# The mLSTM input projection of an encoder layer moved ahead of the attention and computed from the split x

## The reference, cut to what matters

```python
z = x @ w_in + b_in
(a_x, a_g, sb_q, sb_k, sb_v, ml_q, ml_k, ml_v, ml_o, ml_i, ml_f, mg) = jnp.split(z, offs, axis=-1)
# branch A: conv -> RG-LRU(a_x) * gelu(a_g)        branch B: stick-breaking attention(sb_q, sb_k, sb_v)
# branch C: mLSTM(ml_q, ml_k, ml_v, ml_i, ml_f) -> headwise LayerNorm * ml_norm_g * sigmoid(ml_o)
mixed = g[:, :, 0] * (ya @ w_pa) + g[:, :, 1] * (yb @ w_pb) + g[:, :, 2] * (yc @ w_pc)   # g = sigmoid(mg)
x = _layer_norm(DN_ALPHA * x + mixed @ w_out, ln1_g, ln1_b)
```

## Time and profile before

| what | value |
|---|---|
| median of 3 runs | 2867.72 us (2865.27 to 2868.11) |
| the profiled execution's own time | 2888.07 us |
| its span | 2886.3 us |
| TensorE (PE) busy | 2605.4 us, 90% of the span |
| VectorE (DVE) / ScalarE (ACT) / GpSimd (POOL) busy | 1564.3 / 1324.7 / 624.7 us |
| mean granted TensorE clock | 0.952 of full speed |
| data moved | 442.00 MB, 153 GB/s |

### The profile page before, as it was taken

The page is one execution under the profiler, slowest core; times in us unless marked ns, Lnnn a source line. Parts: engine busy times, 40 slices in busy tenths (PEclk is TensorE's granted clock), DMA queues, the critical chain, the costliest instruction groups (busy, mean ns, idle before and its releaser), DMA issues. The chain is left out here.

```text
span 2886.3 us, 40166 instructions
## 1 busy us (share of the span) xinstructions
PE 2605.4 (90%) x14952; PEld 2256.1 (78%) x14952; DVE 1564.3 (54%) x2508; ACT 1324.7 (46%) x2057; POOL 624.7 (22%) x494
## 2 busy tenths in 40 slices
PE   6997898889999699999989886599999999999991
PEld 5996687654447599999987565499999999899990
DVE  3655215653105644544534364477777777777774
ACT  3665214432013333434332222267677776777762
POOL 1000003301102001011113222133433334343333
PEclk9998899999999799999999888799999999999995
DMA  4110313192001455555534311588888888888864
GB/s 127 53 55 19 122 48 117 56 361 70 0 29 16 88 127 138 143 135 136 139 105 153 116 44 48 180 249 255 276 244 276 257 265 274 247 274 249 276 199 157
DMA packets 372397, 442.00 MB, mean 153 GB/s; under 512 B 20509, under 2 KB 299925, under 8 KB 372282
## 3 DMA queue, kind: packets, MB, share of 16 engines
q1 hardware_dynamic: 352264, 379.29, 42.3%
q0 software_dynamic: 15680, 50.90, 7.4%
q10 hardware_dynamic: 4338, 10.23, 0.9%
HBM read 389.36 MB, written 51.01 MB: 153 GB/s over the span
## 5 line engine op out<-in xcount | busy, mean ns | idle before, releaser
L2979 PE MATMUL banks<-slot_rowsT,expert_w_high 128*128 128x384 f32 x2048 | 603.2, 363 | 0.4 <-DVE slot_rowsT L3080 0.4
L2981 PE MATMUL banks<-slot_rowsT,expert_w_low 128*128 128x192 f32 x2048 | 515.0, 251 | 0.0
L2981 PEld LDWEIGHTS banks<-slot_rowsT,expert_w_low 128*128 128x128 f32 x2048 | 392.3, 192 | 1.3
L2979 PEld LDWEIGHTS banks<-slot_rowsT,expert_w_high 128*128 128x128 f32 x2048 | 385.5, 188 | 2.0 <-issue 0.6
L3015 ACT CAST expert_w_high<-expert_w 128x2048 fp32r<-128x2048 f32 x128 | 238.0, 1908 | 21.2 <-DMA expert_w<-in_exp_w 21.2
L3074 DVE TENSOR_TENSOR expert_w_low<-expert_w,expert_w_high 128x2048 fp32r<-128x2048 f32 x96 | 216.9, 2285 | 22.0 <-ACT expert_w_high L3015 22.0
L2884 POOL TENSOR_TENSOR expert_w_low<-expert_w,expert_w_high 128x2048 fp32r<-128x2048 f32 x32 | 147.6, 4613 | 264.1 <-ACT expert_w_high L3015 264.1
L1926 PE MATMUL banks<-xT_chunk_high,w_gates_high 128*128 128x384 f32 x576 | 193.5, 336 | 11.0 <-DVE xT_chunk_low L1992 11.0
L1927 PE MATMUL banks<-xT_chunk_low,w_gates_high 128*128 128x384 f32 x576 | 193.3, 336 | 0.0
L1928 PE MATMUL banks<-xT_chunk_high,w_gates_low 128*128 128x384 f32 x576 | 193.3, 336 | 0.0
L3140 DVE TENSOR_TENSOR expert_w_low<-expert_w,expert_w_high 128x1024 fp32r<-128x1024 f32 x128 | 157.0, 1227 | 54.4 <-ACT expert_w_high L3044 53.5
(11 more groups left out here) (482 smaller groups left out, 6043.7 us busy)
## 6 DMA issues: line engine op xcount, KB each, us to landing
expert_w<-in_exp_w SPq DMA_DIRECT2D x128, 1024.0 KB
expert_w<-in_exp_w SPq DMA_DIRECT2D x32, 2048.0 KB, 10.8
w_gates<-in_w_in SPq DMA_DIRECT2D x72, 512.0 KB, 4.5
cached_k<-in_cache_sb_k SPq DMA_DIRECT2D x16, 1024.0 KB, 9.0
cached_v<-in_cache_sb_v SPq DMA_DIRECT2D x16, 1024.0 KB, 10.9
w_proj<-in_w_pa SPq DMA_DIRECT2D x24, 512.0 KB, 5.2
w_ax_ag<-in_w_in SPq DMA_DIRECT2D x16, 512.0 KB, 4.7
w_sb_piece<-in_w_in SPq DMA_DIRECT2D x24, 256.0 KB, 3.7
```

The source lines that it names most:

```text
L2979: nc.tensor.matmul(out[:, 0:2 * SLOTS], hi, xgT[:, par, k].rearrange("p a s -> p (a s)"), start=(k == 0), stop=(k == DT - 1), skip_group_c ...
L2981: last = nc.tensor.matmul(out[:, 0:SLOTS], lo, xgT[:, par, k, 0, :], start=False, stop=(k == DT - 1), skip_group_check=True)
```

## The change

The mLSTM projection is moved to directly behind `stage_lru`, where `x_hi` and `x_lo` are still in SBUF, and works in three-term products. Its outputs go to DRAM scratch (q and k^T by feature, k, v and o by token) and `stage_mlstm` loads them back in four groups of tiles. The second load and turn of x are gone. For the merge gates GpSimd adds `x_hi` and `x_lo` during `stage_lru` and stores the sum to DRAM (`xT_d`), and `stage_mix` loads it by chunks into one buffer `xa` that later in the chunk holds `ya`. The blank halves of `qz` and the ones of `v_aug` are written by VectorE at the start of `stage_mlstm`.

```diff
 def stage_lru(nc, g, x_hi, x_lo, xT):
...
+            for k in range(DT):
+                if k >= H:
+                    pool.wait_ge(x_out[k % H], 16)
+                pool.tensor_tensor(xT[:, k % H, :], x_hi[:, k, :].bitcast(F32), x_lo[:, k, :].bitcast(F32), ALU.add
+                                   ).then_inc(x_joined, 1)
+                pool.wait_ge(x_joined, k + 1)
+                pool.dma_start(g.xT_d[k], xT[:, k % H, :]).then_inc(x_out[k % H], 16)
...
+def stage_ml_project(nc, g, x_hi, x_lo, turn, m):
+    pieces = [(s, k) for s in range(3) for k in range(DT)]
+    offs = (O_MO, O_MQ, O_MV)
+    RAW, WR, NBK, R = 4, 12, 6, 3
+    QK = [(c, tile) for c in range(len(CHUNKS3)) for tile in (2, 3, 0, 1)]
...
+        GATE_PARTS = (((0, 384), (384, 768)), ((768, 960), (960, T)))
...
+            for n in range(DT, WR + RAW):
+                load(n)
+            for i in range(NT - 1):
+                store_o(i)
+            sp.wait_ge(m_ready, 1)
...
+            for n in range(WR + RAW, 2 * DT + RAW):
+                load(n)
+            store_o(NT - 1)
+            for c in range(2):
+                store_features(c)
+            for n in range(2 * DT + RAW, 3 * DT):
+                load(n)
+            store_features(2)
...
+            for i in range(NT):
+                sp.wait_ge(tok_moved, NT + i + 1)
+                sp.dma_start(g.mv_d[i], tok[:, (NT + i) % R, :]).then_inc(tok_out[(NT + i) % R], 16)
...
+            for i in range(NT):
+                token_rows(0, i, i)
+                if 1 <= i <= 2:
+                    gates(i - 1)
+            for u, (c, tile) in enumerate(QK):
...
+                if u == 2:
+                    turn_gates()
+                if u % 4 == 3:
...
+                    for i in range(3 * c, 3 * c + 3):
+                        turn_k(i)
+            for i in range(NT):
+                token_rows(2, NT + NQK + i, i)
...
+        @block.vector
...
+            for t in range(NT - 1):
+                move(t)
+                if t == 2:
+                    running_rows()
+                if t == 4:
+                    exponents()
+            for n in range(WR, 2 * DT + 4):
+                weight_low(n)
...
+        @block.scalar
...
+            for i in range(2, 5):
+                sigmoid(i)
+            act.wait_ge(rows_ready, 1)
...
+            for i in range(5, NT - 1):
+                sigmoid(i)
+            for n in range(WR, 2 * DT + 4):
+                weight_high(n)
...
-class XRows:
-def stage_turn_rows(nc, g, rows, rows_in, xT):
-def stage_ml_project(nc, g, xT, m):
...
 def stage_mlstm(nc, g, m, ycT):
+        GROUPS = ((0, 1), (1, 3), (3, 6), (6, NT))
...
+            for n, (first, end) in enumerate(GROUPS):
+                cols = slice(first * P, end * P)
+                for half in range(2):
+                    r = slice(64 * half, 64 * half + 64)
+                    sp.dma_start(m.qz[r, half::2, cols], g.mq_d.rearrange("a p t -> p a t")[r, :, cols]
+                                 ).then_inc(tiles_in[n], 16)
+                sp.dma_start(m.kT[:, :, cols], g.mkT_d.rearrange("a p t -> p a t")[:, :, cols]
+                             ).then_inc(tiles_in[n], 16)
+                sp.dma_start(m.k_tok[:, first:end, :], g.mk_d.rearrange("i p d -> p i d")[:, first:end, :]
+                             ).then_inc(tiles_in[n], 16)
+                for i in range(first, end):
+                    last = sp.dma_start(m.v_aug[:, i, :, 0:HD], g.mv_d[i].rearrange("p (h e) -> p h e", h=H))
+                    last.then_inc(tiles_in[n], 16)
...
+                tiles_loaded(pe, i)
+                if i < 2:
+                    pe.wait_ge(blank, 2 + 2 * i)
...
 def stage_mix(nc, g, mixT, yb, yc):
                 sp.dma_start(wg[:, n % 2], w_in_t[:, :, O_MG + r * D + m * P:O_MG + r * D + (m + 1) * P]
                              ).then_inc(wg_in[n % 2], 16)
+                if n == 0:
+                    load_x(0)
...
+                if n % U == 2 * DT + 2 and c + 1 < C:
+                    sp.wait_ge(y_split, 4 * H * (c + 1))
+                    load_x(c + 1)
                 if n % U == 3:
-                    if c:
-                        sp.wait_ge(y_split, 4 * H * c)
-                    sp.dma_start(ya[:], g.yaT_d.rearrange("k p t -> p k t")[:, :, c * CHUNK3:(c + 1) * CHUNK3]
+                    sp.wait_ge(x_split, DT * (c + 1))
+                    sp.dma_start(xa[:], g.yaT_d.rearrange("k p t -> p k t")[:, :, c * CHUNK3:(c + 1) * CHUNK3]
                                 ).then_inc(ya_in, 16)
```

More of the change, by code:

```diff
@@ L308, in stage_lru @@
         states_out = sem("a_states_out")
+        x_joined = sem("a_x_joined")
+        x_out = [sem(f"a_x_out{i}") for i in range(H)]
         block = ctx.enter_context(nc.Block())
@@ L1588, in stage_mlstm @@
         seg = sb("request_mask", [P, NB])
+        GROUPS = ((0, 1), (1, 3), (3, 6), (6, NT))
+        group_of = [n for n, (lo, hi) in enumerate(GROUPS) for i in range(lo, hi)]
+        tiles_in = [sem(f"r_tiles_in{n}") for n in range(len(GROUPS))]
+        o_in = sem("r_o_in")
+        blank = sem("r_blank")
+        ones_ready = sem("r_ones_ready")
         c_in = sem("r_c_in")
@@ L1794, in new_state @@
                 last.then_inc(c_ready, 1)
+            for cols in (slice(0, P), slice(P, T)):
+                for half in range(2):
+                    nc.vector.memset(m.qz[64 - 64 * half:128 - 64 * half, half::2, cols], 0.0).then_inc(blank, 1)
+            nc.vector.memset(m.v_aug[:, :, :, HD:HD + 1], 1.0).then_inc(ones_ready, 1)
             for i in range(NT):
@@ L1896, in _, with load_x @@
             w_in_t = g.w_in[0].rearrange("(k p) n -> p k n", p=P)
+            def load_x(c):
+                for half in range(2):
+                    k = slice(4 * half, 4 * half + 4)
+                    sp.dma_start(xa[:, k, :], g.xT_d.rearrange("k p t -> p k t")[:, k, c * CHUNK3:(c + 1) * CHUNK3]
+                                 ).then_inc(x_in[half], 16)
             for n, (c, r, m) in enumerate(units):
@@ L2025, in _ @@
                 first = n % U < DT
-                if first:
-                    dve.wait_ge(x_split, DT * (c + 1))
                 out = mixT[:, m, c * CHUNK3:(c + 1) * CHUNK3] if first else sig[:, n % RING, :]
@@ L3310, in build_program @@
                     prompt.close()
[L3311 to L3315 removed]
+                    stage_sb_sample(nc, g, qT, k_new, v_new, cache)
                 cache.close()
```

629 lines of the change are left out of this document (354 added, 275 removed).

## The result

The kernel after takes 2830.82 us (median of 4 runs, 2828.16 to 2833.89), the kernel before in the same batch 2867.91 us (4 runs). The ratio is 0.9874, 95% interval 0.9861 to 0.9886: faster by 37.1 us. The forecast was 2830.0 us, range 2816 to 2851. The profiled execution took 2832.34 us, with a span of 2830.6.

The account below looks back on a forecast made before the run. TensorE, busy 90% of the span, bounds dense stretches; stage edges count elsewhere. -231.0 + 183.8 + 1.5 + 4 + 4 = -37.7 us; against the median of 2867.72 that gives 2830 us, range 2816 to 2851.

Parts of the forecast that it names:

- Removed and added: Second turn of x and float32 projection go, -231.0 us; the new projection stage before the attention costs 183.8 us.
- The late gate chain: New projection stage: ScalarE's casts come in time by 1 to 2 us; rival: late, +8 us, 2838, chance 0.12.
- GpSimd in the LRU stage: LRU stage: eight GpSimd additions slow two or three VectorE operations by 0.5 us each, +1.5 us.
- the lock rival: LRU stage: GpSimd's additions lock VectorE out, at most five on the path, +13.5 us for 1.5, 2842; chance 0.08.
- Start of the mLSTM stage: mLSTM stage: first reload group takes 5 to 7.5 us before score matmuls, +4 us, ends 0 and 10.
- Start of the mix: Mix: 1.5 MB of x stand ahead of the first projection weights, +4 us, between +2 and +8.
- Slow reloads: Rival, mLSTM stage: q, k, v reloads crawl at 50 GB/s, 61 us for 4, 2887; chance 0.10.

Follow-up runs that it names:

- second profiles: Kernel before and kernel after each run once more unchanged, for a second profile: 2868.37 us and 2831.95 us.
- experiment 7: Kernel after with additions spread over the LRU stage, mix's first projection weights ahead of x, and four casts ahead of the gates' exponentials: 2823.13 us.
- experiment 4: Kernel after with a GpSimd memset of 2.68 us in place of each addition, storing only the high part of x: 2830.12 us in one run.
- experiment 2: Kernel after with each GpSimd addition held back until an LRU output tile is done, spreading them over the stage: 2825.40 us, ratio to before 0.9851.
- experiment 3: Kernel after without GpSimd's additions, storing only the high part of x: 2826.09 us, ratio 0.9861.
- experiment 6: Kernel after with the mix's first projection weights issued ahead of the first chunk of x: 2829.82 us, ratio 0.9867.
- experiment 1: Kernel before plus only GpSimd's eight additions and their stores in the LRU stage, result unread: 2875.32 us against 2868.52, ratio 1.0024.

## Why the prediction was right

The sum was -37.7 us and the runs gave -37.1, but it is a hit in which some of the terms missed and made up for each other. The terms against both pairs of profiles, in us (the mix is taken up to the next stage's first issue; the 22.75 us of the late weights are taken off the first pair's later stages):

| | forecast | first profiles | second profiles |
|---|---|---|---|
| LRU stage | +1.5 | +9.4 | +8.8 |
| new projection | +183.8 | +184.9 | +184.9 |
| attention | 0 | +1.6 | +0.5 |
| second turn and float32 projection | -231.0 | -231.0 | -233.0 |
| mLSTM stage | +4 | +1.4 | -1.6 |
| mix | +4 | +3.8 | +4.3 |
| later stages | 0 | -3.1 | -0.3 |
| sum | -37.7 | -33.0 | -36.4 |

Term by term, against the first profiles where nothing else is said:

- **Removed and added: right.** -231.0 stands. The new stage was put at 183.8 us and takes 184.9. Its parts: start 4.2 us for 4.4; first nine tiles and gates 66.2 for 66.6; features with the turns and waits 60.9 for 59.3; last nine tiles 49.6 for 48.6; end 4.1 for 4.4. The rows of the attention's own projection are good prices for the new one.
- **The late gate chain: nearly free.** I gave a margin of 1 to 2 us and no cost. The group row of the new stage shows a wait of 1.4 us at the first feature unit:

```profile
L796 PE MATMUL banks<-xT_high,w_ml_high 128*128 128x384 f32 x96 | 33.6, 350 | 1.4 <-DVE w_ml_low L826 1.4
```

  ScalarE reached the casts 66.6 us after the first matmul, where I had 66; TensorE's fifth piece would have been wanted at 68.3 instead of 69.4 and came 0.5 us late, the sixth 0.9. (The forecast's own numbers, 66.6 and twelve matmuls of 175 ns, give 68.7 and not 69.4.) With four casts ahead of the exponentials (experiment 7) the wait is gone. The loss of 8 us was never near.
- **GpSimd in the LRU stage: the step that failed.** "Two or three VectorE operations on that path at 0.5 us each give +1.5 us" should have read: each is shut out until GpSimd's whole instruction ends, up to 2.7 us, and TensorE, idle for 6.8 us, comes back at half clock. The stage grew by 9.4 us for 1.5; by the experiments 5 to 7 us of that reach the time. VectorE operations of over 2.5 us early in this stage were named beforehand as the sign of a wrong step, and they are there. The mechanism is that of the lock rival, which had a chance of 0.08; its price of 13.5 us was too high, as the rows shut out on the convolution's path add up to 6 us, with 2.8 us of half clock behind them. I called the row beside it, 0.5 us longer at the median, milder than the rule of the Trainium skill's page (experiment 4), and I took from that rule only the operations with two SBUF inputs, while two of the three stretched rows have a single tensor as input. The row is not milder. The operations beside that row in the trace of before show why:

```profile
1105.43 1.02 POOL L2039 TENSOR_TENSOR xT<-xT,gate_sigmoid 128x384 f32<-128x384 f32 x1 [7.04 <-DVE gate_sigmoid L2030]
...
1105.81 1.72 DVE L2008 TENSOR_TENSOR w_gates_low<-w_gates,w_gates_high 128x1024 fp32r<-128x1024 f32 x1 [0.46 <-ACT w_gates_high L1962]
```

  GpSimd's addition there is of 384 columns and 1.02 us long, and 0.64 us of it were left when the split began. The split lost 0.5 us because little more was left to wait for; beside an addition of 2.7 us the same wait is up to 2.7 us. The units of the mix without an addition have splits of 1.22 us. A loss per operation can't be carried over to another stage without the length of what stood beside it.
- **Start of the mLSTM stage: the loads cost little.** I took +4 us for 4.48 to 8.5 us up to the first score matmul. They began 5.95 us in, 7.04 in the second profile, against 4.48 and 5.66 in the two of before. In its first 5 us TensorE has sixteen small matmuls that need no load, in either kernel, and only what comes after them waits for one. That wait is none in the first profile of after, 1.17 us in the second, 0.2 to 1.1 in experiments 2, 3 and 6:

```profile
848.53 2.08 PE L1787 MATMUL banks<-ycT,ml_kT 128*128 128x128 f32 x8 [1.17 <-DMA ml_v<-ml_v_scratch]
```

  So of the 1.4 us between the second profiles 1.2 are this wait. Of the 1.5 us between the first profiles it is nothing: there the small matmuls take 5.8 us at half clock and took 4.4 us in the kernel before, where they began at full clock. The stage takes 109.5 and 110.0 us after, 108.05 and 111.56 before: the change costs between -2.1 and +1.9 us, by which pair one takes.
- **Start of the mix: right.** +4 forecast, +4.1 measured, from 7.97 to 12.09 (+3.4 in the second profiles, from 7.96 to 11.40), by the very order of the list. The x chunk and the weights behind it arrive by 962.4.
- **Slow reloads: wrong rival.** 268 GB/s.

The two pairs differ by 3.4 us in the sum, and the two profiles of before reach the mix 5.9 us apart. That is more than the 0.6 us by which the forecast missed the runs, so such a hit is partly luck: 7 to 8 us of the LRU stage were missed, and 3 to 6 us that the mLSTM stage did not cost, with what the other stages differ by between executions, made up for them. What was shown is the new stage's price, the loss in the LRU stage, and the mix's start.

## What to carry to other kernels

Price a new stage by the twin that already stands in the trace, down to start and end; that held within 1.1 us of 184. When work is moved to GpSimd because it is idle, look at what VectorE does in the same microseconds and not at the shares of the stage: three small operations that each waited for one GpSimd instruction cost TensorE 6.6 us and then 2.8 us of half clock, of which 5 to 7 us reached the time. The remedy is a place in time (experiment 2) rather than another engine, and it costs one wait.

## Unexpected behaviour of the hardware

- A VectorE multiply of 128 columns, 0.34 us by itself, took 2.98 us beside a GpSimd addition, and 3.10 us beside a GpSimd memset that reads nothing. Beside that same memset, a split with two inputs took its normal 1.23 us.
- The wait goes the other way, too. In experiment 2 the first six additions took 3.55 us each, and each began 0.2 us after a VectorE split of 1.22 us with two inputs (91.55 after 91.38, 119.61 after 119.43). The last two, with no split beside them, took 2.64 and 2.69 us. The splits kept their 1.22 us.
- A row's start does not tell who came first: in experiment 1 the copy of 54.93 began, by the profile, 0.37 us before the addition of 55.30, and yet ended with it at 58.03 (0.17 us is its usual length).
- Two profiles of the same kernel had granted clocks of 0.66 and 0.51 in the same ten us, and the stage was 3.5 us longer.
